# A two-layer-path Hyena/RG-LRU block on one core: the index exchanges of the long convolution go through DRAM instead of through TensorE

## What is computed

```python
xn = rms_norm(x, g_norm1) * (1 + scale1) + shift1          # modulation from silu(c) @ w_ada
proj = xn @ w_in                                            # x_r, y_r, and v, x1, x2 (512 channels each)
...                                                         # RG-LRU group on x_r, y_r
k_f = hyena_filter_fft(L, ...)                              # sin-MLP over positions, decay window, rfft
def fft_long_conv(u, k_f, bias):                            # twice, one after the other
    U = rfft(u, n=2 * L, axis=1)
    return irfft(U * k_f, n=2 * L, axis=1)[:, :L] + u * bias
z = x1 * fft_long_conv(v, k_f[:, 0], hy_bias[0])
z = x2 * fft_long_conv(z, k_f[:, 1], hy_bias[1])
o = concat(rms_norm(o_r), rms_norm(z)) @ w_out              # then a gated conv FFN
```

## Time and profile before

| | us |
|---|---|
| median of 3 runs | 3153.41 (3149.79 to 3155.58) |
| the profiled execution | 3151.1 |
| its span | 3149.1 |
| in_proj | 0 to 648 |
| hyena, first filter alone | 648 to 686.6 |
| hyena, eight turns | 686.6 to 1274 |
| out_and_up, ffn_down | 1274 to 3149 |

### The profile page before, as it was taken

How to read it: one execution, slowest core, us unless ns; L and a number is a source line. 1 busy time by engine, 2 the same in 40 slices (tenths; PEclk the granted TensorE clock), 3 DMA queues, 4 the chain that set the end, 5 groups by cost and what they waited for, 6 DMA issues and landing times. The chain is left out here.

```text
span 3149.1 us, 40467 instructions
## 1 busy us (share of the span) xinstructions
PE 2945.6 (94%) x16404; PEld 2548.6 (81%) x16404; DVE 1696.4 (54%) x1888; ACT 930.5 (30%) x1608; POOL 669.3 (21%) x344
## 2 busy tenths in 40 slices
PE   5999999979999998598899999999999999999998
PEld 2778787878999888577788888888888887788886
DVE  6754664546666666465564565565565563322223
ACT  5443434135555555354511101100100103211111
POOL 3132333102222222244222222222222210000000
PEclk7999999989999999799999999999999999999999
DMA  6211221422121211434411111101111105322222
GB/s 228 68 58 63 79 79 63 123 117 86 56 86 56 86 56 55 135 127 155 160 35 55 48 34 55 48 34 55 48 34 55 48 22 187 123 75 75 82 87 72
DMA packets 92739, 252.84 MB, mean 80 GB/s; under 512 B 14846, under 2 KB 53246, under 8 KB 83198
## 3 DMA queue, kind: packets, MB, share of 16 engines
q1 hardware_dynamic: 92608, 251.00, 23.4%
HBM read 175.01 MB, written 75.96 MB: 80 GB/s over the span
## 5 line engine op out<-in xcount | busy, mean ns | idle before, releaser
L1783 PE MATMUL out_up_banks<-xh_rest,up_w_hi 128*128 128x512 f32 (+2 forms) x1408 | 492.6, 350 | 10.5 <-DVE xl_rest L1893 8.4
L1783 PE MATMUL out_up_banks<-xh_rest,up_w_lo 128*128 128x512 f32 (+2 forms) x1408 | 493.0, 350 | 0.0
L1783 PE MATMUL out_up_banks<-xl_rest,up_w_hi 128*128 128x512 f32 (+2 forms) x1408 | 492.6, 350 | 0.0
L1939 DVE SCALAR_TENSOR_TENSOR ffn_hidden<-grid,params,ffn_hidden 128x2048 f32<-128x2048 f32 x176 | 457.7, 2601 | 24.6 <-DVE ffn_hidden L1936 0.2
L2095 PE MATMUL down_banks<-down_hi,down_h_hi 128*128 128x512 f32 x748 | 293.8, 393 | 10.9 <-DVE down_gate L2176 4.9
L1783 PEld LDWEIGHTS out_up_banks<-xh_rest,up_w_hi 128*128 128x128 f32 x1408 | 266.0, 189 | 41.9 <-DVE xl_rest L1893 9.3
L2095 PE MATMUL down_banks<-down_lo,down_h_hi 128*128 128x512 f32 x748 | 293.0, 392 | 0.0
L2095 PE MATMUL down_banks<-down_hi,down_h_lo 128*128 128x512 f32 x748 | 292.5, 391 | 0.0
L1783 PEld LDWEIGHTS out_up_banks<-xl_rest,up_w_hi 128*128 128x128 f32 x1408 | 265.7, 189 | 30.5
L136 POOL TENSOR_TENSOR up_w_hi<-up_w_whole,zero 128x1024 fp32r<-128x1024 f32 x44 | 124.1, 2820 | 779.2 <-PE out_up_banks L1783 762.4
L1783 PEld LDWEIGHTS out_up_banks<-xh_rest,up_w_lo 128*128 128x128 f32 x1408 | 265.8, 189 | 28.1
(11 more groups left out here) (262 smaller groups left out, 5692.2 us busy)
## 6 DMA issues: line engine op xcount, KB each, us to landing
hidden_ff_dram<-ffn_hidden SPq DMA_DIRECT2D x22, 1088.0 KB, 4.8
up_w_whole<-w_up_in SPq DMA_DIRECT2D x44, 512.0 KB, 5.2
pre_dram<-in_result SPq DMA_DIRECT2D x16, 1088.0 KB, 4.0
down_h<-hidden_ff_dram SPq DMA_DIRECT2D x88, 192.0 KB, 2.3
wada_late<-w_ada_late_in SPq DMA_DIRECT2D x32, 512.0 KB, 3.7
down_x<-w_down_in SPq DMA_DIRECT2D x22, 512.0 KB, 4.0
in_w_whole<-w_in_in SPq DMA_DIRECT2D x20, 512.0 KB, 4.4
home<-x_rows_in SPq DMA_DIRECT2D x17, 512.0 KB, 6.8
```

What stands on the lines that cost most here:

```text
L1783: last = pe.matmul(out, weight[:, u, k], in_block(value, rest, b, k), start=(k == 0 and j == 0), stop=(k == KM - 1 and j == 2))
L1939: last = nc.vector.scalar_tensor_tensor(out=y, in0=window, scalar=weight, in1=y, op0=ALU.mult, op1=ALU.add)
```

## The change

In hyena the three exchanges are no longer transposes. After `first`, `back1` and `f_first`, ScalarE evicts the bank into one of four buffers (`hy_sent`, `f_sent`); SyncE *sends* that buffer (256 KB, 2 KB a partition) to DRAM, and *fetches* it two batches later into 16 partitions of `hy_spectrum`, `hy_pairs` or `f_spectrum`, with the index exchanged (512-byte pieces). A fetch waits on SyncE for its send to have landed. The next transform waits for all eight fetches. `first` and `f_first` now hold the table still and stream 512 columns of data, one matmul a batch, and `back1` has its operands turned as well. `turn_back`, `turn_pairs` and `f_turn_back` and their evictions are gone. `hy_swapped` and `taps` now lie in `hy_rows`.

The order is new: per turn the list is `SEND_FIRST` (turn_rows and first, alone), `SEND_FILTER` (taps and f_first of the next turn, context, one ada), `SEND_BACK` (second and back1, one ada, and the large loads as `bulk` in its middle), six f_second with two ada and ctx_back, back2, then two f_second and ctx_filter. The store of z, the gates, v, decay and w3 loads stand in that list too.

In in_proj the last MLP pieces are spread over the first token block, rows 8 to 11 are loaded earlier, the splits of the first two weight units move in GpSimd's order, some buffers are placed elsewhere, and mean and scaling of the next block stand within the loop of pieces from the second block on.

The diff, cut to its core:

```diff
+                for t in range(8, 12):
+                    load_row(t)
...
-                for n in range(len(flat) + 4):
+                for n in range(8):
...
+                        if b == 0 and k in (1, 3):
+                            sine(5 + k // 2)
+                            scale_angle(8 + k // 2)
+                        if b == 0 and k in (5, 6):
+                            sine(7 + k - 5)
...
+                        if b == 0 and k in (2, 3):
+                            subtract_turns(4 + k)
+                        if b == 0 and k in (3, 5):
+                            count_turns(8 + k // 4)
+                        if b == 0 and k == 6:
+                            subtract_turns(8)
+                        if b and b + 1 < NB and k == 5:
+                            mean(b + 1)
+                        if b and b + 1 < NB and k == 6:
+                            scale_rows(b + 1)
+                    if b == 0:
+                        subtract_turns(9)
+                        mean(1)
+                        scale_rows(1)
...
-                            for step in todo[:2]:
-                                first_product(*step)
-                            todo = todo[2:]
+                        if b == 0 and k in (2, 5):
+                            mlp(8 + k // 5)
+                        for step in todo[:1]:
+                            first_product(*step)
+                        todo = todo[1:]
...
+def moved(stages, *names):
+    out = []
+    for stage, j in stages:
+        out.append((stage, j))
+        if stage in names:
+            out.append((stage + "_send", j))
+            if j >= 2:
+                out.append((stage + "_fetch", j - 2))
+            if j == 7:
+                out += [(stage + "_fetch", 6), (stage + "_fetch", 7)]
...
+CONV_FIRST = (numbered("turn_rows", 0, 1) + numbered("first", 0, 1) + numbered("turn_rows", 2) + numbered("first", 2, 3)
+              + numbered("turn_rows", 3) + numbered("first", 4, 5, 6, 7))
+CONV_MIDDLE = (numbered("second", 0, 1, 2, 3) + [x for j in range(4) for x in (("back1", j), ("second", j + 4))]
+               + numbered("back1", 4, 5, 6, 7))
+CONV_LAST = numbered("back2", 0, 1, 2, 3)
+FILTER_FIRST, FILTER_SECOND = one_ahead("taps", "f_first"), numbered("f_second", *range(8))
+CONV_CHAIN = CONV_FIRST + CONV_MIDDLE + CONV_LAST
+FILTER_CHAIN = FILTER_FIRST + FILTER_SECOND
...
+SEND_FIRST = moved(CONV_FIRST, "first")
+SEND_BACK_ONLY = interleave(moved(CONV_MIDDLE, "back1"), [("bulk", 0)])
+SEND_FILTER = interleave(moved(FILTER_FIRST, "f_first"), [("ctx_turn", 0), ("ctx_taps", 0), ("ctx_forward", 0)] + ada(0))
+SEND_BACK = interleave(moved(CONV_MIDDLE, "back1"), [("bulk", 0)] + ada(1))
+FILTER_ONCE = interleave(moved(FILTER_FIRST, "f_first"), [("ctx_taps", 0)])
+BOTH = ([("store", 0)] + SEND_FILTER + SEND_BACK
+        + interleave(FILTER_SECOND[:6], ada(2) + ada(3) + [("ctx_back", 0)]) + CONV_LAST
+        + interleave(FILTER_SECOND[6:], [("ctx_filter", 0)]))
+ONLY_CONV = ([("ctx_turn", 0), ("ctx_forward", 0)] + ada(0) + ada(1) + SEND_BACK_ONLY
+             + ada(2) + ada(3) + [("ctx_back", 0)] + CONV_LAST)
+
...
+def across(rows):
+    return rows.rearrange("(k s) i c -> (s i) k c", s=4)
...
+        swapped = rows[:, 8:].rearrange("p (j q) c -> p j q c", q=4)
+        gated = swapped.rearrange("p j q c -> p j (q c)")
+        taps = rows[:, :8].rearrange("p (j q) c -> p j q c", q=4)
...
+            for stage, j in FILTER_ONCE:
                 batch(stage, j, 0, 0, None, 0)
-            for ct in range(CT - 1):
-                for order in range(2):
-                    for stage, j in BOTH:
-                        batch(stage, j, ct, order, ct * 2 + order, ct * 2 + (order + 1))
-            for order in range(2):
-                for stage, j in (BOTH, ONLY_CONV)[order]:
-                    batch(stage, j, CT - 1, order, 2 * (CT - 1) + order, 2 * (CT - 1) + order + 1)
+            for stage, j in SEND_FIRST:
+                batch(stage, j, 0, 0, 0, 1)
+            for stage, j in FILTER_SECOND + [("ctx_filter", 0)]:
+                batch(stage, j, 0, 0, None, 0)
+            for turn in range(2 * CT):
+                ct, order = divmod(turn, 2)
+                for stage, j in (SEND_FIRST if turn else []) + (BOTH if turn < 2 * CT - 1 else ONLY_CONV):
...
+                def batch(stage, j, ct, order, turn, f_turn):
+                    if stage in ("first_send", "back1_send"):
+                        stage = stage[:-5]
+                        sp.wait_ge(out[stage], turn * 8 + j + 1)
+                        sp.dma_start(d["swap_" + stage][j], sent[:, j % 4]).then_inc(sent_done[j % 4], 16)
+                    elif stage == "f_first_send":
+                        sp.wait_ge(out["f_first"], f_turn * 8 + j + 1)
+                        sp.dma_start(d["swap_f_first"][j], f_sent[:, j % 4]).then_inc(f_sent_done[j % 4], 16)
+                    elif stage == "first_fetch":
+                        sp.wait_ge(sent_done[j % 4], sends_before("first", j, turn, f_turn) * 16 + 16)
+                        sp.dma_start(spectrum[SLOT_ROWS[j]:P:8], across(d["swap_first"][j])).then_inc(spectrum_loaded, 16)
+                    elif stage == "back1_fetch":
+                        sp.wait_ge(sent_done[j % 4], sends_before("back1", j, turn, f_turn) * 16 + 16)
+                        sp.dma_start(pairs[SLOT_ROWS[j]:P:8], across(d["swap_back1"][j])).then_inc(pairs_loaded, 16)
+                    elif stage == "f_first_fetch":
+                        sp.wait_ge(f_sent_done[j % 4], sends_before("f_first", j, turn, f_turn) * 16 + 16)
+                        sp.dma_start(f_spectrum[SLOT_ROWS[j]:P:8],
+                                     across(d["swap_f_first"][j])).then_inc(f_spectrum_loaded, 16)
+                    elif stage == "store":
+                        if order == 0 and ct:
+                            wait_for_turn(turn - 1)
+                            store_z(ct - 1)
+                    elif stage == "bulk":
+                        if order == 1:
+                            wait_for_turn(turn - 1)
+                            load_gates(ct, 1)
+                            if ct + 1 < CT:
+                                load_v(ct + 1)
+                        else:
+                            if ct:
+                                sp.wait_ge(z_stored, ct * 16)
+                                load_gates(ct, 0)
+                            if ct + 1 < CT:
+                                sp.wait_ge(out["taps"], ct * 16 + 16)
+                                sp.wait_ge(out["ctx_taps"], ct * 2 + 2)
+                                load_filter_inputs(ct + 1)
+                    elif stage == "ada_load":
+                        load_ada(LATE_PER_TURN * turn + 2 + j)
+
...
-                        if j == 0:
-                            if order == 0:
-                                pe.wait_ge(v_loaded, ct * 16 + 16)
-                            else:
-                                pe.wait_ge(out["back2"], turn * 4 + 4)
+                        if order == 0:
+                            pe.wait_ge(v_loaded, ct * 16 + 16)
+                        else:
+                            pe.wait_ge(out["back2"], turn * 4 + j // 2 + 3)
...
-                        for q in range(2):
-                            last = pe.matmul(bank[:, 256 * q:256 * q + 256], rows[:, 2 * j + q], first_t[:],
-                                             start=True, stop=True)
+                            pe.wait_ge(first_loaded, 16)
+                        last = pe.matmul(bank, first_t[:, j % 2], rows[:, j // 2 * 4:j // 2 * 4 + 4]
+                                         .rearrange("p s c -> p (s c)"), start=True, stop=True)
+                    elif stage == "second":
                         if j == 0:
-                            pe.wait_ge(out["first"], turn * 8 + 8)
+                            pe.wait_ge(spectrum_loaded, turn * 128 + 128)
...
-                        pe.wait_ge(out["turn_pairs"], turn * 8 + 2 * j + 2)
+                            pe.wait_ge(pairs_loaded, turn * 128 + 128)
                         for q in range(8):
-                            last = pe.matmul(bank[:, 64 * q:64 * q + 64], spectrum_p[:, 8 * j + q], back2_t[:],
+                            last = pe.matmul(bank[:, 64 * q:64 * q + 64], pairs[:, 8 * j + q], back2_t[:],
...
+                        last = pe.matmul(bank, f_first_t[:], taps[:, j % 2].rearrange("p q c -> p (q c)"),
+                                         start=True, stop=True)
+                    elif stage == "f_second":
+                        if j == 0:
+                            pe.wait_ge(f_spectrum_loaded, f_turn * 128 + 128)
+                        if turn is None and j == 0:
...
-                        nc.scalar.activation(spectrum_c[:, 8 * j:8 * j + 8, :].rearrange("p r b -> p (r b)"), bank,
```

(5 more changed lines are left out.)

310 lines of the change are left out of this document (133 added, 177 removed).

## The result

The changed kernel takes 3178.34 us (median of 5 runs, 3173.69 to 3187.91) against 3152.25 (5 runs) for the kernel before: a ratio of 1.0086, 95% interval 1.0074 to 1.0098. The prediction had 3127 and called it faster; it is slower by 27 us. 3178 lies within the range of 3075 to 3185, near its upper end, but on the side that the prediction thought the less likely one. Most of the loss hangs on large loads that stand ahead of back1's sends on SyncE's list.

The account below looks back on a forecast made before the run. TensorE, busy 94%, was taken as the bound. Hyena's 20 us and in_proj's 6 us off 3151.1 gave 3125, or 3127 as median of runs; range 3075 to 3185, the forecast alone 3106 to 3148.

Parts of the forecast that it names:

- A: First phase of a hyena turn, turn_rows and first alone: 11.7 us, 3 of it for ScalarE's remaining evictions.
- B: Phase of taps and f_first of the next filter: 17.7 us, 2 of it waiting for VectorE's context block; covers first's exchange.
- E: Phase of back2 in a hyena turn: 7.5 us.
- F: Phase of two f_second and ctx_filter at a turn's end: 2.7 us, with GpSimd's last gating hidden.
- T: Length of a hyena turn: 73 us, 3.2 less than before; the slow rival decides from 76.6.
- The last turn: Hyena's final turn: 55 us, as before, with 6 us for back1's exchange and 9.5 for back2 and the gate.
- the exchange of back1 in D: Back1's send and fetch: over 0.7 + 5.7 us after the phase starts, covered unless loads stand before it.
- D: Phase of six f_second, two ada and ctx_back: near 9 us, plus 1.5 (0 to 8) for the large loads.
- C: Phase of second and back1: 19.2 us, first result after 4.5, then seven rounds of 1.93 us, 13.5 in all.
- Rival 3: Back1's exchange stands bare at the first back2, sends late behind bulk loads: turn 81 us, time 3183, chance 0.20.
- Rival 4: TensorE's clock falls to 0.5 for stretches in a turn with waits in every phase: turn 80 us, 3176, chance 0.08.
- Rival 2: Phases of a turn overlap better, waits and small gaps go: turn 65 us, hyena 550, time 3071, chance 0.27.

Follow-up runs that it names:

- r4: The changed kernel with its large loads spread over the turn (ahead of back2, after the last batch, behind first) instead of in back1's stretch: 3156.1 us, ratio 1.0017.
- r5: r4 with each load of late ada weights placed right behind its own ada product: 3138.2 us, ratio 0.9957.
- r7: The changed kernel with each fetch reading one 16 KB stretch of DRAM per partition instead of 32 pieces of 512 bytes: 3169.0 us, ratio 1.0057.
- r8: The changed kernel with back1's fetches reading the long-stored copy of first's exchange, so not waiting for their own sends: 3166.2 us, ratio 1.0043.
- r3: The changed kernel with each load of late ada weights right behind the ada product that frees its buffer: 3193.3 us, ratio 1.013.
- r14: The changed kernel with the eviction to ada_rows done by VectorE instead of ScalarE: 3178.2 us, ratio 1.0068.
- r2: The changed kernel with hyena's large loads (decay, gates and v after the first) moving only 64 KB each, at the same places: 3144.2 us, ratio 0.998.
- r9: The changed kernel with its large loads moved from ahead of back1's first send to the middle of second/back1: 3190.3 us, ratio 1.0119.
- r12: The changed kernel with f_second moved behind first, taps and f_first behind back1, v loaded with the gates, filter inputs at the end of even turns: 3130.1 us, ratio 0.9928.

## Why the prediction was wrong, point by point

**Right.** A at 10.6 and B at 17.8 us (11.7, 17.7), though B partly by luck: no wait for `taps` is left in it, for which it had 2 us, and waits for `f_sent` (5.3 us in three of the six turns), which it hadn't, are. E and F. That first's exchange is covered by B: second waits for DMA in the last turn only. That f_first's sends queue behind the tables at the start (11.9 us, forecast "to about 672", measured until 665.9). The share of the rings, 0.77 for "near 0.7". The break-even point of T = 76.6 was too high: r4 at T = 74.8 is about equal to the kernel before, though it has the 9.5 us of in_proj, r5 at 72.8 is faster, r7 and r8 at 77 are slower by 0.4 to 0.6%. The start and the last turn, below, cost more than was carried.

**The ledger.** Hyena was to take 95.3 + 7 x 73 = 606.3 us and took 665.5 (639.9 to 1305.4), 59.2 more. Turns 1 to 6: 6 x 5.64 = 33.9. Turn 0 after its A: 64.9 for 61.3, 3.6. The start: 56.2 for 52, 4.2. The last turn: 72.6 for 55, 17.6. in_proj gave 8.7 us up to hyena's start for 6. The stretch 80 to 90 is busy 7.3 of 10 us with the change, for 4.3.

**The step that failed is the exchange of back1 in D**: "back1's exchange is over 0.7 + 5.7 us after D starts: covered, unless loads stand before it", and for the loads "I put 1.5 us a turn on that (0 to 8)". Measured: it ends 16.9 us after D starts, and D is 8.3 us over its 10.5. Three things were wrong in it.
- The loads were priced at 1.5 us a turn. They stand ahead of back1's first send, which then lands 13.3 us after its issue (2.4 forecast). ScalarE's slots, the fetches, the ada weights and the last send all wait behind it, so one delay shows in three waits. Take one away and the next takes over: r3 removes the wait for the weights, r14 that for `ada_rows`, r8 that of the fetches for their sends, and D stays at 16.2, 17.7 and 17.0. Take the bytes (r2) or their place (r4, r5) away and D falls to 12.8, 12.3 and 10.8. I had followed the exchange and not `ada_load`, and so missed the waits that TensorE's list meets first; but by the landings they cost only 1.2 to 2.7 us a turn beyond the exchange's own lateness. The sum of the two ada waits follows the time in most runs (r4 26 us at 3156, r8 48 at 3166, r7 49 at 3169, the changed kernel 55 and r14 55 at 3178, r9 72 at 3190), but not in r3 (30 at 3193).
- The latencies were those of an empty list, 2.3 to 2.6 us. In the changed kernel 256 KB land in 3.8 to 5.7. I had worked out a load of 50 to 70 us of a turn, and then used times from rings at 0.26. Even with r2's small loads the exchange ends 11.5 us after D begins and D is 12.8. The estimate of 2.6 us for one DMA, from the Trainium skill (DMA: Bandwidth & Descriptors, section Anatomy of one DMA), is what the rows of the kernel before show; the landings here disagree once the queue is loaded, and the measurement decides.
- The place of bulk was misread. By r9 that made the forecast no worse.

**C** is 2.6 us over. The first back1 comes 5.6 us after the first second, not 4.5, and the ring of second, swap, GpSimd, add doesn't keep its 1.93 us, which the prediction had named as a sign of being wrong. GpSimd's first and last multiplication of turn 2:

```profile
872.99 2.49 POOL L1324 TENSOR_TENSOR hy_rows<-hy_rows,filter_im 128x512 f32<-128x512 f32 x2 [33.89 <-ACT hy_rows L1277]
...
888.05 1.36 POOL L1324 TENSOR_TENSOR hy_rows<-hy_rows,filter_im 128x512 f32<-128x512 f32 x1 [0.57 <-ACT hy_rows L1277]
```

Seven rounds take 15.1 us for 13.5, in steps of 1.2 and 3.2 by turns and then 1.8 to 2.5. In the last turn they are 1.92 us apart. Why the steps alternate was not settled.

**The last turn** was "55, as now" with 6 us for back1's exchange. TensorE waits 4.4 us for first's exchange and 8.5 for back1's, and back2 then runs at half clock, 13.9 for 7.1 us. That is 6.8 of the 17.6; the waits are 4.4 and 8.5 - 6 = 2.5; four second batches at 6.75 instead of 3.8 are 3.0 more; 16.7 together.

**The rivals.** Rival 3 was right, in the time almost (T = 81, 3183) and in its mechanism: sends queued behind the bulk loads land late, SyncE waits for each, and the lateness adds up until back1's exchange isn't covered. Its sign, a wait of back2, shows in the last turn only, since the waits for ada stand ahead of back2 in TensorE's list; r3, without the wait for the weights, shows it in six. Rival 4, the clock, is in it: it is 0.67 in the D above. It follows the waits there; where they go, in r12's turn, it is 0.97. The Trainium skill (TensorE: Matmul & The Clock Gate, section Part 1) has idle time lower the clock; the D above agrees, and r3's back2 (0.51 with TensorE busy throughout) shows a phase without waits at the lower level behind one with them. Rival 2's time, 3071, needed T = 65; the best order found has 72.3.

## What to carry to other kernels

When transfers go onto a queue that was nearly idle, read its whole list again, not only the new exchange: here three loads ahead of the first send made everything behind them late. Price a landing by what stands ahead of it: the same 256 KB send took 5.7 us behind large loads and 2.7 in r12, with the rings about equally busy. A view of waits names what an engine's list meets first; before you price the removal of a wait, read when the next thing in the list would have been ready (here 1.2 to 2.7 us earlier). Put large loads where no send follows soon: with the order of the stages unchanged, their place and that of the ada weights took the kernel from 3178 to 3138 us. A longer phase in front of the exchange as well gave 3130.
